# Eight direct SBUF transfers in place of a DRAM scratch, each way, for 16 x 16 blocks of a triangular inverse

## The reference

```python
    def step(S, inp):
        r_t, w_t, k_t, v_t, kk_t, a_t = inp
        sa = jnp.einsum('bhvk,bhk->bhv', S, -kk_t)
        S = S * w_t[:, :, None, :] + sa[..., None] * (kk_t * a_t)[:, :, None, :] + v_t[..., None] * k_t[:, :, None, :]
        return S, jnp.einsum('bhvk,bhk->bhv', S, r_t)
```

## Time and profile before

| | us |
|---|---|
| median of 3 runs | 1674.34 (1672.53 to 1674.45) |
| the profiled execution, its own time | 1671.37 |
| its span in the profile | 1669.6 |
| PE busy in the span | 1613.1 (97%) |
| DVE busy | 1249.7 |
| ACT busy | 993.3 |
| POOL busy | 74.1 |

### The profile page before, as it was taken

How to read it: one execution, slowest core, us unless ns; L and a number is a source line. 1 busy time by engine, 2 the same in 40 slices (tenths; PEclk the granted TensorE clock), 3 DMA queues, 4 the chain that set the end, 5 groups by cost and what they waited for, 6 DMA issues and landing times.

```text
span 1669.6 us, 25177 instructions
## 1 busy us (share of the span) xinstructions
PE 1613.1 (97%) x9482; PEld 1366.1 (82%) x9482; DVE 1249.7 (75%) x1160; ACT 993.3 (59%) x944; POOL 74.1 (4%) x176
## 2 busy tenths in 40 slices
PE   9999979999999999997999999999999999999997
PEld 8979768778887997876878888888888888888886
DVE  5765855664446677494478899898988889898987
ACT  5554443454444654362446777777777777777775
POOL 0030120000000030102000000000000000000000
PEclk9999989999999999998999999999999999999999
DMA  9444433655554643533368999999999999899993
GB/s 296 140 146 134 125 127 102 221 176 178 197 180 153 202 153 105 154 126 106 122 237 282 348 376 381 328 364 340 393 329 370 373 336 395 325 362 330 391 380 138
DMA packets 217712, 414.03 MB, mean 248 GB/s; under 512 B 10144, under 2 KB 84256, under 8 KB 217120
## 3 DMA queue, kind: packets, MB, share of 16 engines
q1 hardware_dynamic: 213840, 400.97, 67.7%
q10 hardware_dynamic: 2256, 8.82, 1.4%
q0 software_dynamic: 1536, 3.15, 0.9%
HBM read 408.18 MB, written 2.62 MB: 246 GB/s over the span
## 4 chain that ended last, share of the span: by engine, by line
PE 79%; DVE 8%; DMA 4%; issue 3%; POOL 3%; ACT 2%; SPq 0%; DVEq 0%; ACTq 0%; POOLq 0%
PE W L523 17%; PE W L525 16%; PE W L524 16%; PE Y L523 7%; PE Y L525 7%; PE Y L524 7%; PE Y L816 2%; PE W L721 1%; POOL own L1805 1%; POOL step L1801 1%; DVE w_lo L1863 1%; DMA raw<-w_in 1%; DVE sc L2008 1%; DMA own<-blocks_in 1%; DMA blocks_in<-diag 1%
## 5 line engine op out<-in xcount | busy, mean ns | idle before, releaser
L523 PE MATMUL W<-w_lo,x_hi 128*128 128x512 f32 (+1 forms) x1168 | 452.1, 387 | 1.5 <-DVE x_lo L2197 0.9
L525 PE MATMUL W<-w_hi,x_hi 128*128 128x512 f32 (+1 forms) x1168 | 442.4, 379 | 0.0
L524 PE MATMUL W<-w_hi,x_lo 128*128 128x512 f32 (+1 forms) x1168 | 441.9, 378 | 0.0
L1863 DVE TENSOR_TENSOR w_lo<-raw,w_hi 128x2048 fp32r<-128x2048 f32 x112 | 256.9, 2295 | 183.3 <-ACT w_hi L1303 182.0
L1870 DVE TENSOR_TENSOR w_lo<-raw,w_hi 128x2048 fp32r<-128x2048 f32 x144 | 329.6, 2289 | 45.7 <-ACT w_hi L1309 45.7
L1309 ACT ACTIVATE w_hi<-raw 128x2048 fp32r<-128x2048 f32 x144 | 276.0, 1917 | 72.6 <-PE Y L525 40.1
L1870 DVE TENSOR_TENSOR w_lo<-raw_more,w_hi 128x2048 fp32r<-128x2048 f32 x120 | 274.9, 2291 | 28.3 <-ACT w_hi L1309 27.6
L1309 ACT ACTIVATE w_hi<-raw_more 128x2048 fp32r<-128x2048 f32 x120 | 230.5, 1921 | 64.8 <-PE W L525 42.0
L1303 ACT ACTIVATE w_hi<-raw 128x2048 fp32r<-128x2048 f32 x112 | 214.2, 1913 | 75.1 <-PE W L525 39.5
L523 PEld LDWEIGHTS W<-w_lo,x_hi 128*128 128x128 f32 x1168 | 220.2, 189 | 44.9 <-issue 4.8
L525 PEld LDWEIGHTS W<-w_hi,x_hi 128*128 128x128 f32 x1168 | 220.0, 188 | 42.2
(11 more groups left out here) (351 smaller groups left out, 1800.4 us busy)
## 6 DMA issues: line engine op xcount, KB each, us to landing
raw<-w_in SPq DMA_DIRECT2D x123, 512.0 KB, 4.5
raw<-moe_gate SPq DMA_DIRECT2D x48, 1024.0 KB, 6.6
raw<-moe_up SPq DMA_DIRECT2D x48, 1024.0 KB, 7.4
raw<-moe_down SPq DMA_DIRECT2D x48, 1024.0 KB, 5.6
raw_more<-moe_gate SPq DMA_DIRECT2D x40, 1024.0 KB, 7.4
raw_more<-moe_up SPq DMA_DIRECT2D x40, 1024.0 KB, 7.4
raw_more<-moe_down SPq DMA_DIRECT2D x40, 1024.0 KB, 6.4
raw<-w_branch SPq DMA_DIRECT2D x24, 512.0 KB, 4.3
```

The source lines that it names most:

```text
L523: nc.tensor.matmul(out_ap, lhs[0], rhs[1], start=start, stop=False)
L524: nc.tensor.matmul(out_ap, lhs[1], rhs[0], start=False, stop=False)
L525: return nc.tensor.matmul(out_ap, lhs[0], rhs[0], start=False, stop=stop)
L1863: V.tensor_tensor(w_lo[u % 3][:], raw[u % 3][:], w_hi[u % 3][:].bitcast(F32), ALU.subtract)\
```

## The change

The two scratch tensors go. Block rows travel from SBUF to SBUF directly, one transfer for each u: eight into `own`, eight into `solved`. The transfer for u takes 128 partitions x 16 numbers of `diag` and writes 8 partitions x 256 numbers of `own`, 8 KB in 128 runs of 64 bytes; the way back is the reverse. All eight are issued one after the other on GpSimd's queue; GpSimd waits once for the eight into `own`, DVE once for the eight into `solved`. The numbers moved and the inversion between are the same.

```diff
@@ -276,7 +276,6 @@
-        blocks_in, blocks_out = (nc.dram_tensor(name, (8, P, BS), F32, kind="Internal").ap() for name in ("blocks_in", "blocks_out"))
@@ -290,12 +289,6 @@
-        def by_row(ap):
-            return ap.rearrange("u j t -> j u t")
-
-        def by_block(ap):
-            return ap.rearrange("u (b j) t -> (u b) (j t)", j=BS)
@@ -1783,18 +1776,17 @@
-            def moved(n, leg):
-                pool.wait_ge(sem("blocks_moved"), 16 * (4 * n + leg))
+            def matrices(u):
+                return own[2 * NB * u:2 * NB * (u + 1), :, :]
 
             def solve(l, p):
 
                 n = 2 * l + p
                 made = SOLVED * n + 1
                 pool.wait_ge(sem("blocks_made"), made)
-                pool.dma_start(by_row(blocks_in), diag[:]).then_inc(sem("blocks_moved"), 16)
-                moved(n, 1)
-                pool.dma_start(own[:].rearrange("p j t -> p (j t)"), by_block(blocks_in)).then_inc(sem("blocks_moved"), 16)
-                moved(n, 2)
+                for u in range(8):
+                    pool.dma_start(matrices(u), diag[:, u, :]).then_inc(sem("blocks_moved"), 16)
+                pool.wait_ge(sem("blocks_moved"), 16 * (16 * n + 8))
...
                 pool.wait_ge(sem("blocks_made"), SOLVED * (n + 1))
-                pool.dma_start(by_block(blocks_out), own[:].rearrange("p j t -> p (j t)")).then_inc(sem("blocks_moved"), 16)
-                moved(n, 3)
-                pool.dma_start(solved[:], by_row(blocks_out)).then_inc(sem("blocks_moved"), 16)
+                for u in range(8):
+                    pool.dma_start(solved[:, u, :], matrices(u)).then_inc(sem("blocks_moved"), 16)
@@ -2024,7 +2015,7 @@
-                dve.wait_ge(sem("blocks_moved"), 16 * (4 * n + 4))
+                dve.wait_ge(sem("blocks_moved"), 16 * (16 * n + 16))
```

## The result

The changed kernel takes 1680.97 us (median of 6 runs, 1678.28 to 1682.02); the kernel before, beside it, 1673.22 us (6 runs). The ratio is 1.0044, 95% interval 1.0032 to 1.0057: 7.75 us slower. The profiled execution took 1681.84 us with a span of 1680.0.

What follows compares the result with a forecast made beforehand. PE bounds the kernel, losing time in its waits for `xt`. Ways out in passes 2 and 4 +0.66 and +0.72, passes 1 and 3 -0.87 and -1.18, ways in 0: -0.67 us, giving 1673.6 us, range 1669.0 to 1681.0.

Steps and rivals of the forecast that it cites:

- What bounds: Whole kernel: time is won or lost in PE's four waits for DVE's `xt`, 28.8 us in all.
- (a): Both ways: one GpSimd issue of 128 runs of 64 bytes takes 0.56 us, between 0.49 and 0.93.
- (b): Both ways: the last transfer takes 2.0 us from issue to landing; a way with idle DMA engines takes 5.9 us.
- (c): Ways in beside the weight stream: the eighth transfer lands at the same 228.0, so no change in any pass.
- R3: Ways in: held transfers land one after another, about 1 us more each; total +2.7, 1677.0 us; chance 0.15.
- The sum for pass 1: Way out of pass 1: 7.23 - 5.92 = 1.31 us to gain, capped at 0.87.
- R1: Both ways: issues cost 0.72 us or more, the last queued behind the second weight pair; 1694 to 1704 us; chance 0.12.
- R2: Both ways: the eight transfers don't overlap, 15.2 us each way; 1743 us; chance 0.01.
- R4: After PE's waits in passes 1 and 3 the clock may not fall, giving back 4.3 us: 1669.3 us; chance 0.12.

Runs made afterwards that it cites:

- e7: The changed kernel with sixteen transfers of half the size (64 runs of 64 bytes) on the way out in place of eight; 1702.86 us in a single run.
- e3: The changed kernel, but SP issues the weight pair that ran beside the way in only when `own` is filled; 1672.07 us, ratio to before 0.9996.
- e6: The changed kernel, but SP issues the weight pair beside the end of the way out in passes 1 and 3 only when `solved` is filled; 1678.01 us.
- e2: The kernel before with only the way out by eight direct transfers, the way in still through the DRAM scratch; 1673.25 us, ratio to before 0.9999.
- e5: As e4, but SP issues its four way-in transfers as soon as `diag` is ready, ahead of its wait for the weight split; 1664.08 us, ratio to before 0.9951.
- e4: The changed kernel with each eight split: four on GpSimd, four on SP (way in) or ACT (way out); 1664.95 us, ratio to before 0.9956.
- e8: The changed kernel, but only the second weight pair of each way in waits until `own` is filled; 1680.86 us, ratio to before 1.0048.
- e1: The kernel before with only the way in by eight direct transfers, the way out still through the DRAM scratch; 1678.8 us, ratio to before 1.0032.

## Why the prediction was wrong

The measured 1680.97 us lies at the very end of the range, 1681.0, but the forecast was "no change, 0.7 us faster", and the kernel is slower beyond doubt. That the time is inside the range at all is luck: its upper end stood for transfers held by the stream and one way in caught by a second pair; what came was the first of these and a way out that was caught. Step by step:

- **What bounds.** Right. PE's four waits for `xt` hold +8.2 of the 10.4 us between the two profiled executions.
- **(a) Price of an issue.** 0.56 taken, 0.594 measured, the line through the two of the earlier trace rows gave 0.57. The small miss is 0.24 us a way. The line has the price grow with the runs; e7 shows no growth from 64 to 128 (0.605 and 0.594, where the line has 0.546 and 0.571).
- **(b) Last landing with idle engines.** 2.0 taken, 1.93 to 2.02 measured (changed kernel and e3). So the way out of passes 2 and 4 is 6.2 us to `xt` for the 5.9 + 0.1 of the sum, and the losses there are +0.8 and +0.9 for +0.66 and +0.72.
- **(c) Way in: no change in any pass.** This is the step that failed. I had read from one two-hop case that a small transfer queued beside a weight pair lands 0.7 us after the pair, and took that for eight in a row. They are held, as e3 shows, but don't land together with the end of the pair: in pass 2 the five that were held landed over 2.2 us, where the prediction had the eighth at the same time as the old second hop. The ways in are 1.8, 1.2, 1.1 and 1.3 us longer. In passes 2 and 4 that is 2.5 us on the path, for 0 forecast. It is rival R3, given 0.15 and priced at 1 us a way.
- **The sum for pass 1.** A gain of 0.87 was forecast, a loss of 4.2 came. The way out was costed with the issue times of the trace of before. The way in had moved it by 1.5 us, the last issue came at 106.20 instead of about 104.8, and SP's next pair, itself 0.5 us earlier than before (105.90 for 106.40), was on the way by then. By e6 this cost 2.4 to 3.0 us of time and 4.1 us of PE's wait (3.96 for 8.03). I had asked of the ways in what a second pair does to them (R1), and not of the ways out. Pass 3 has the same build and lost nothing: there SP's pair was issued at 640.80, 0.45 us after the last of the eight, which landed in 2.02 us.
- **R1 and R2**, dear issues or none overlapping: no. 0.594 is below the 0.72 at which R1 decides. The rule of the Trainium skill, "DMA: Bandwidth & Descriptors", section "Anatomy of one DMA — SWDGE (gpsimd) path", of about 2.0 us for each transfer holds for the last landing (1.96) and not for a row of them: 6.2 us for eight.
- **R4, the clock.** The waits came down to 3.0 to 3.25 us in seven cases: passes 1 and 3 of e2, e3 and e5, and pass 1 of e4. The mean granted clock in the 10 us after them was 1.00 in two (pass 3 of e3, pass 1 of e4) and 0.83 to 0.84 in five. So such a wait can spare the fall, but it doesn't by itself, and a gain from it can't be counted on.

The clock also takes part in the 10.4 us. Stretches of 10 us from the first product, PE busy throughout; the third number from the right is the mean granted clock. Kernel before, passes 1 and 3, then the changed kernel, the same:

```profile
108.45:118.45 10.00, 10.00 (x102) 8.28 (x103) 6.59 (x11) 5.21 (x7) 0.00 (x0) 0.83 0.27 92
635.32:645.32 10.00, 10.00 (x97) 8.27 (x98) 6.20 (x11) 5.21 (x7) 0.00 (x0) 0.69 0.22 78
```

```profile
112.15:122.15 10.00, 10.00 (x97) 8.24 (x98) 6.20 (x11) 5.21 (x7) 0.00 (x0) 0.70 0.01 2
642.94:652.94 10.00, 10.00 (x102) 8.24 (x103) 6.95 (x11) 5.21 (x7) 0.00 (x0) 0.83 0.24 85
```

A mean of 0.83 leaves (1 - 0.83) x 10 = 1.7 us of full-speed work undone. By this estimate pass 1 of the changed kernel lost 1.3 us more than before to the clock and pass 3 lost 1.4 less. The trace bears it out: from the first product of pass 1 to that of pass 2 the changed kernel took 3.4 us more, 2.1 of them the longer wait; from pass 3 to pass 4 it took 0.8 more, though the wait grew by 2.1. What is left, +1.3 and -1.2, agrees with the clock's +1.3 and -1.4. After pass 4 about 2 us were lost, most of them in a stretch where the clock was 0.83 (878.44 to 908.44) and before 0.89 (870 to 900): 30 x 0.06 = 1.8 us. e3 has the 0.83 there too (865 to 895) and e8 the 0.89 (875 to 905), so I don't put it down to the change; no run was made for it.

## What to carry to other kernels

A row of small transfers on one queue costs its issues: count them, times the measured price, plus one landing. Two hops through DRAM are 5.3 us here and hard to beat with eight issues at 0.6; with four on each of two queues they are beaten. When a chain of small transfers is moved in time, lay its new issue times beside the times at which the big stream is issued, for every later transfer of the chain too: issued 0.45 us before a weight pair a transfer landed in 2.0 us, issued 0.27 us before it in 3.0 to 3.5, 0.11 before in 4.3, and 0.30 after its first issue in 5.4.

## What was not expected of the hardware

- The price of an issue on GpSimd was the same for half the runs: 0.594 us with 128 runs of 64 bytes, 0.605 with 64. On SP and ACT the same transfer takes 0.65 and 0.64 us (four in 2.58 and 2.56), no less than on GpSimd.
- DVE's `w_lo` subtraction holds a tensor operation of GpSimd until it ends (0.20 us became 1.87), but not an issue: the eight issues of passes 1 to 3 of the changed kernel began inside one and took 4.72 to 4.89 us. "SBUF — State Buffer" in the Trainium skill, section "SBUF: two separate sides", lets a DVE operation with two SBUF inputs shut out a GpSimd operation that reads SBUF; rows of e5 agree.
- GpSimd paused in pass 4 for 1.16 to 1.17 us after the sixth of eight issues, in the changed kernel, e3, e6 and e8 alike, at the same place of the program, and not in e1. In e7 the pause came after the first issue of the way out of passes 3 and 4, 0.89 and 1.45 us. Why isn't known. In the changed kernel the way in of pass 4, held anyway, was no longer for it (8.38 us); in e3 it was 1.1 us longer.
- The small transfers also slow the big ones: in pass 2 a weight pair issued in the midst of eight landed in 4.7 us (mean of the two), beside two hops in 4.1.
